# A two-layer hybrid decoder in fp32: one more FFN tile by seven products, the gate unit in two passes, and four changed orders

## What is computed

```python
def hybrid_layer(x, ...):
    h = rmsnorm(x, norm_mix)
    z = h @ w_in
    (rq, rk, rv, rg, pu, mq, mk, mv, mo, mi, mf) = jnp.split(z, offs, axis=-1)
    y_ret = retention(rq, rk, rv, rg, positions, ret_gn)
    y_pool = pool_mix(pu, pool_w, pool_scale)
    y_ml = mlstm(mq, mk, mv, mo, mi, mf, conv_w, conv_b, b_igate, b_fgate, mlstm_gn)
    x = x + jnp.concatenate([y_ret, y_pool, y_ml], axis=-1) @ w_out
    h = rmsnorm(x, norm_ffn)
    gu = h @ w_gate_up
    x = x + (jax.nn.silu(gu[..., :D_FF]) * gu[..., D_FF:]) @ w_down
    hp = rmsnorm(x, norm_ple)
    x = x + jax.nn.sigmoid(hp @ w_ple_gate) * (p_i @ w_ple_proj)
    return x
```

## Time and profile before

| | us |
|---|---|
| three runs | 2525.21, 2525.93, 2527.05 |
| median | 2525.93 |
| the profiled execution | 2527.18 |
| its span, first to last instruction | 2525.1 |
| PE busy (matmul) | 2485.7 |
| POOL busy | 992.1 |
| DVE busy | 1238.0 |
| ACT busy | 853.7 |

### The profile page before, as it was taken

How to read it: one execution, slowest core, us unless ns; L and a number is a source line. 1 busy time by engine, 2 the same in 40 slices (tenths; PEclk the granted TensorE clock), 3 DMA queues, 4 the chain that set the end, 5 groups by cost and what they waited for, 6 DMA issues and landing times.

```text
span 2525.1 us, 29697 instructions
## 1 busy us (share of the span) xinstructions
PE 2485.7 (98%) x11844; PEld 2052.7 (81%) x11844; DVE 1238.0 (49%) x1746; ACT 853.7 (34%) x1237; POOL 992.1 (39%) x596
## 2 busy tenths in 40 slices
PE   7999999999999999999999999999999999999997
PEld 5888788888888878888888888888888888888885
DVE  7856756454333352332585667546443333423335
ACT  4221225433333341234333121334333333322253
POOL 3211112177788742212121111222877887222220
PEclk9999999999999999999999999999999999999998
DMA  4322223122322252311142112311223223422111
GB/s 157 93 67 51 71 63 109 34 92 76 96 79 76 82 202 80 104 50 50 42 145 80 51 47 67 101 60 66 76 76 95 80 76 101 164 104 73 51 50 67
DMA packets 62904, 208.64 MB, mean 83 GB/s; under 512 B 8872, under 2 KB 17320, under 8 KB 58416
## 3 DMA queue, kind: packets, MB, share of 16 engines
q1 hardware_dynamic: 34848, 120.60, 15.2%
q10 hardware_dynamic: 27920, 86.16, 9.9%
HBM read 161.08 MB, written 32.54 MB: 77 GB/s over the span
## 4 chain that ended last, share of the span: by engine, by line
PE 97%; DVE 1%; ACT 1%; DMA 1%; issue 0%; POOL 0%; ACTq 0%; DVEq 0%; POOLq 0%
PE proj L1908 20%; PE proj L1910 20%; PE proj L1909 20%; PE proj L2002 5%; PE proj L2004 5%; PE proj L2003 5%; PE aux L2002 5%; PE aux L2004 5%; PE aux L2003 5%; PE aux L2046 1%; PE aux L2146 1%; PE aux L2137 1%; PE aux L2127 0%; PE aux L2232 0%; PE aux L2237 0%
## 5 line engine op out<-in xcount | busy, mean ns | idle before, releaser
L1859 POOL TENSOR_TENSOR w_lo<-w_raw,w_hi 128x1024 fp32r<-128x1024 f32 (+1 forms) x145 | 366.9, 2531 | 1312.2 <-ACT w_hi L1440 1312.0
L1908 PE MATMUL proj<-h_hi,w_hi 128*128 128x512 f32 x1792 | 711.9, 397 | 12.8 <-DVE h_lo L612 12.8
L1909 PE MATMUL proj<-h_hi,w_lo 128*128 128x512 f32 x1792 | 700.5, 391 | 0.0
L1910 PE MATMUL proj<-h_lo,w_hi 128*128 128x512 f32 x1792 | 700.4, 391 | 0.0
L1908 PEld LDWEIGHTS proj<-h_hi,w_hi 128*128 128x128 f32 x1792 | 338.2, 189 | 86.8 <-issue 16.5
L1909 PEld LDWEIGHTS proj<-h_hi,w_lo 128*128 128x128 f32 x1792 | 338.4, 189 | 71.8 <-issue 3.4
L1910 PEld LDWEIGHTS proj<-h_lo,w_hi 128*128 128x128 f32 x1792 | 338.1, 189 | 71.0
L1440 ACT ACTIVATE w_hi<-w_raw 128x1024 fp32r<-128x1024 f32 (+1 forms) x143 | 147.0, 1030 | 448.2 <-PE proj L1910 340.3
L1001 DVE TENSOR_TENSOR x<-x,proj 128x512 f32<-128x512 f32 x128 | 87.7, 687 | 407.3 <-PE proj L1910 407.1
L1866 POOL TENSOR_TENSOR w_lo<-w_raw,w_hi 128x512 fp32r<-128x512 f32 x120 | 183.6, 1531 | 88.5 <-ACT w_hi L1426 88.5
L1866 POOL TENSOR_TENSOR w_lo<-turns,w_hi 128x512 fp32r<-128x512 f32 x120 | 180.4, 1504 | 62.9 <-ACT w_hi L1426 62.9
(11 more groups left out here) (280 smaller groups left out, 4052.1 us busy)
## 6 DMA issues: line engine op xcount, KB each, us to landing
w_raw<-weights SPq DMA_DIRECT2D x170, 512.0 KB, 3.7
act_spill<-act ACTq DMA_DIRECT2D x44, 512.0 KB, 5.5
turns<-weights SPq DMA_DIRECT2D x40, 512.0 KB, 4.3
h_whole<-act_spill ACTq DMA_DIRECT2D x12, 1024.0 KB, 8.5
ffn_b_whole<-act_spill ACTq DMA_DIRECT2D x8, 1024.0 KB, 5.8
w_raw<-weights SPq DMA_DIRECT2D x16, 384.0 KB, 3.1
rows<-ret_qkv ACTq DMA_DIRECT2D x40, 128.0 KB, 2.3
x<-x_in ACTq DMA_DIRECT2D x8, 512.0 KB, 8.5
```

The lines of the kernel that those rows point to most:

```text
L1859: g.tensor_tensor(wlo[:, slot, 0:n], w, whi[:, slot, 0:n].bitcast(F32), ALU.subtract).then_inc(weights_ready.sem, 1)
L1908: pe.matmul(out, wh, rhi, start=first, stop=False)
L1909: pe.matmul(out, wl, rhi, start=False, stop=False)
L1910: return pe.matmul(out, wh, rlo, start=False, stop=final)
```

## The change

- **FFN.** `NSTD` goes from 2 to 1, so that 21 tiles are blocks. Block 0 now comes after one plain tile. Its tile of raw weights comes from the two `turns` slots, and the three banks of block 0 are those of `aux` in place of `proj`. An odd number of blocks leaves one half slot of the ring out at the start.
- **Third token sum.** DVE makes `t3` and the low parts of sum 1 ahead of `plain_up`. ACT makes the high parts of the fourth sum, and of operands 4 and 5, after the first product of block 0.
- **Gate unit.** Unit 0's weights have 64 columns at most, so the low parts are put into the columns 64 to 127 of `w_hi` (`gate_low`), and `two_passes` multiplies both with `h_hi` and then with `h_lo`. PSUM then has two parts, which DVE reads in two instructions and adds in a third.
- **Four orders.** POOL's split of unit 2 waits for the sum of squares in place of `h_lo`; ACT's high parts of activations 2 and 3 in the last block come one product later; the last token sum is made by PE from the sum of the first squares and the last two squares themselves; and DVE's adding of those two goes.

The core of the diff:

```diff
-NSTD = 2
+NSTD = 1
@@ plan_weights
             if u == U_DN:
+                block_turn = 2 * (NBS % 2)
+                at += NBS % 2
@@ vector, evacuate
                 if u == U_GATES:
-                    src, scale, dst = src[0:64], scale[0:64], mix[0:64, 0, sl]
+                    v.tensor_tensor(mix[0:64, 0, sl], src[0:64], scale[0:64], ALU.mult).then_inc(vec_step.sem, 1)
+                    step_at(L)
+                    src, scale, dst = src[64:128], scale[64:128], mix[0:64, 2, sl]
@@ vector, gate_rows_1
+                v.tensor_tensor(mix[0:64, 0, :], mix[0:64, 0, :], mix[0:64, 2, :], ALU.add).then_inc(vec_step.sem, 1)
@@ vector, ple_gates, last layer
                     gate_out(L, 15)
-                    gate_square(L, 14)
-                    gate_square(L, 15)
@@ vector, ffn
                         t_low(L, 0, 1)
+                        t3(L)
+                        t_low(L, 1, 0)
                         plain_up(L, 0)
-                        t_low(L, 1, 0)
-                        t3(L)
                         t_low(L, 2, 2)
-                        plain_gate(L, 1)
-                        plain_up(L, 1)
                         t_low(L, 3, 3)
@@ scalar, ffn_blocks
+                        if k == 0:
+                            a.wait_ge(unit_done.sem, unit_done.at(L, U_DN))
+                            t_high(L, 3, 3, 8)
+                            highs_ahead(L, 4)
+                            highs_ahead(L, 5)
...
-                        if last and 2 <= i <= 5:
-                            act_high(L, 2 * i - 4)
-                            act_high(L, 2 * i - 3)
+                        if last:
+                            for f in {2: (0, 1), 4: (2, 3, 4, 5), 5: (6, 7)}.get(i, ()):
+                                act_high(L, f)
@@ scalar, ffn
-                        units_high(L, U_FFN + 2)
                         t_high(L, 0, 1, 4)
                         plain_silu(L, 0)
-                        units_high(L, U_FFN + 3)
+                        highs_ahead(L, 0)
+                        highs_ahead(L, 1)
                         t_high(L, 1, 0, 0)
                         t_high(L, 2, 2, 12)
...
                         highs_ahead(L, 2)
                         highs_ahead(L, 3)
@@ gpsimd, split
+            def gate_low(hi, whole):
+                hi3 = hi.rearrange("p (k c) -> p k c", c=P)
+                whole3 = whole.rearrange("p (k c) -> p k c", c=P)
+                return g.tensor_tensor(hi3[:, :, 64:128], whole3[:, :, 0:64], hi3[:, :, 0:64].bitcast(F32), ALU.subtract)
...
                     if u == RING - 1:
-                        g.wait_ge(first_lo, KC)
+                        g.wait_ge(first_sum, KC - 1)
@@ tensor
+            def two_passes(out, slot, col, rhi, rlo, first, final):
+                both = whi[:, slot, col:col + P]
+                pe.matmul(out, both, rhi, start=first, stop=False)
+                return pe.matmul(out, both, rlo, start=False, stop=final)
...
+                passes = two_passes if u == U_GATES else three_passes
@@ tensor, end of the program
-            sums(DEPTH, -16, 0, (1,))
+            last_row = ("row", 0, 1)
+            pe.wait_ge(sq_added.sem, sq_added.at(DEPTH, -2))
+            pe.wait_ge(aux_read(last_row), aux_free_at(DEPTH, last_row))
+            pe.matmul(abank(last_row), mean_all, acc[:, 1, :], start=True, stop=False)
+            for j in (14, 15):
+                pe.wait_ge(sq_made.sem, sq_made.at(DEPTH, j - 15))
+                ins = pe.matmul(abank(last_row), mean_all, sqr[:, j % 2, :], start=False, stop=j == 15)
+            ins.then_inc(aux_done.sem, 1)
```

More of the change, by code:

```diff
@@ L185 @@
 AUX, AUX_FILLS, AUX_PER_BANK = plan_aux()
-VEC_STEPS = 271
+VEC_STEPS = 274
 OUT_LAST = [m for m in range(4, KC)] + [m for m in range(4)]
@@ L1496, in ffn_blocks @@
                             a.wait_ge(act_stored.sem, act_stored.at(L, 16 * (NSTD + b - 1)))
-                            a.activation(act_t[:, b % 2, 0, :], x_bank, ACT.Copy).then_inc(copied.sem, 1)
+                            a.activation(act_t[:, (NSTD + b) % 2, 0, :], x_bank, ACT.Copy).then_inc(copied.sem, 1)
+                        if k == 0:
[3 more added lines that the diff above has]
+                            highs_ahead(L, 5)
                         if i == 2:
-                            a.activation(act_t[:, b % 2, 1, :], x_bank, ACT.Copy).then_inc(copied.sem, 1)
+                            a.activation(act_t[:, (NSTD + b) % 2, 1, :], x_bank, ACT.Copy).then_inc(copied.sem, 1)
                         if i == 3:
@@ L1846, in split @@
                         g.wait_ge(first_w, 2 * q + 1)
-                        ins = g.tensor_tensor(wlo[:, 0, hs(q)], w[:, hs(q)], whi[:, 0, hs(q)].bitcast(F32), ALU.subtract)
+                        ins = gate_low(whi[:, 0, hs(q)], w[:, hs(q)])
                         ins.then_inc(first_w if q == 0 else weights_ready.sem, 1)
@@ L1858, in split @@
                     g.wait_ge(unit_hi.sem, unit_hi.at(L, u + 1))
+                if u == U_GATES:
+                    gate_low(whi[:, slot, 0:n], w).then_inc(weights_ready.sem, 1)
+                    return
                 g.tensor_tensor(wlo[:, slot, 0:n], w, whi[:, slot, 0:n].bitcast(F32),
@@ L1917, in product @@
                         ready(i, k)
-                    last = three_passes(out, slot_w, wk + col, rhi(k), rlo(k), i == 0, i == len(ks) - 1)
+                    last = passes(out, slot_w, wk + col, rhi(k), rlo(k), i == 0, i == len(ks) - 1)
                 return last
@@ L2012, in fill_read @@
                     pe.wait_ge(emptied[bank(u, k % 2)].sem, emptied_at(L, u, k % 2))
-                if b == 0:
+                if b == 1:
                     fill_read(0)
-                elif b == 1:
+                elif b == 0:
                     for name in (("row", 1, 0), ("row", 1, 1)):
```

19 lines of the change are left out of this document (6 added, 13 removed).

## The result

The changed kernel takes 2537.96 us (median of 7 runs, 2534.73 to 2541.87); the kernel before, run beside it, took 2527.05 (7 runs, 2523.68 to 2530.87). The ratio is 1.0041, 95% interval 1.0031 to 1.0051: slower by 0.4%. The forecast was 2520, faster. The profiled execution took 2539.96, its span 2538.2, which is 13.1 us over the span before.

The account below looks back on a forecast made before the run. TensorE was taken to bound the kernel, busy 2485.7 of 2525.1 us. From the profiled 2527.2, gains of 14.7 and a new wait of 9.0 gave 2521.5, so about 2520 for the median; range 2508 to 2536.

Parts of the forecast that it names:

- Matmuls removed: Whole kernel: a block has 12 matmuls fewer per layer than a plain tile, 24 x 0.226 = 5.4 us less.
- Start: Start of layer 0: sums of squares no longer held (-3.5), `h_lo` starts earlier (-0.6); together -4.1 us, bounds -3.4 and -7.
- No gain of clock: First token sums of layer 0: PE still waits about 3.6 us, so no gain from its clock was counted.
- Gate unit of layer 1: Layer 1's gate unit: one pass fewer saves 3.6 us, partly lost to waiting; -2.6 us left, bounds -1.5 and -3.6.
- Down projection: Layer 0's down projection: new order of high parts removes PE's wait; -1.8 us, bounds 0 and -2.2.
- End: End of the kernel: DVE's second adding leaves the chain; -0.8 us, bounds 0 and -1.8.
- The new wait: FFN start, block 0: POOL and DVE exclude each other, delaying products; at least 2.5 us, taken as 4.5 per layer, +9.0.
- Rival 1: FFN start: POOL gets the first turn, the two engines alternate, `gate_second` late; 11 us per layer, 2533, slower; chance 0.28.

Follow-up runs that it names:

- kernel 5: Changed kernel with GpSimd's low parts of blocks 0 and 1 and sums of block 1 cut to 64 of 512 columns; 2509.97 us, one execution.
- kernels 1: Changed kernel without its FFN part (`NSTD = 2`, old order at the FFN's start); 2515.61 us, ratio 0.9948 to the kernel before.
- 3: Changed kernel with GpSimd's work on block 1 held until VectorE has made the last low part of block 0's token sums; 2519.12 us, ratio 0.9963.
- 6: Changed kernel with GpSimd's work on block 1 held only until the low parts of the third token sum are made; 2528.33 us, ratio 1.000.
- 8: Kernel before with only GpSimd's split of unit 2 at the start moved behind VectorE's sums of squares; 2520.83 us, one execution.
- 11: Changed kernel with block 1 held behind the fourth token sum and the retention's third unit's low part behind VectorE's eight scalings; 2515.74 us.

## Why the prediction was wrong

It had the right mechanism in a rival and the wrong one in the forecast. For the profiled execution it gave -5.7 and the measurement +13.1, 18.8 apart; 17.8 of these are the one step below that failed. Point by point:

- **Matmuls removed, -5.4: right.** 12 a layer are worth 2.72 (kernel 5), 0.227 each. An estimate by the Trainium skill's figure (TensorE: Matmul & The Clock Gate, Back-to-back issue gap) is 3.1 for both layers. The measurement decides for the row: 5.44.
- **Start, -4.1: right in its two steps, short by the clock.** -4.75 after; the late split by itself -3.6 (the 3.5 of the working), the gates -0.9 (0.6 in the working). "No gain of clock" was wrong: the four token sums took 2.53, where undisturbed ones take 1.88 and three took 2.90 before, 0.9 more was gained behind them in this profile, and 2.5 in others (kernels 1, 3, 6, 8 and 11); with these 2.5 it comes to the bound of -7. The gates' extra VectorE instructions cost nothing that shows.
- **Gate unit of layer 1, -2.6: right.** 1.82 in the turn and 0.62 behind it, 2.4.
- **Down projection, -1.8: right in that profile** (422.63 to 420.65, 2.0). But that wait was not a fixed item of the kernel: with the old order it is 0 to 2 us, from profile to profile.
- **End, -0.8: too small by half.** It gave 1.6. I took only the second adding off the chain and left the first; both squares now go straight from ScalarE into TensorE.
- **The new wait, +4.5 per layer: the step that failed.** It is 13.4 per layer. The text walked the case in which GpSimd is kept out until 510.9, as in the earlier trace rows: one wait of 5.7 at product 3, behind GpSimd's low part, and "later ones hold no more". It took a value between this and the bound (which is 3.1 and not 2.5 by its own numbers: 529.2 + 1.2 - 527.3). The runs showed another path. Product 3 was 1.1 late, and the other 12.3 come behind it, most at the products 5 and 7, which wait for VectorE's `h_lo` and `silu_g`. For GpSimd was not kept out for long: it asked at 502.43, was let in when `t3` began, at 503.7, and from then each engine's next instruction stood ready when the other's ended, up to 534.3, so that four low parts took 6.81 in place of 2.48. I had set a chance of 0.28 on this without asking how long either order lasts: a kept-out run ends with the run, an alternation ends only when one side's work does.
- **Who is let in: not settled.** VectorE's run had no gap at 503.7, so an unbroken run is not what keeps GpSimd out. In the kernel before, GpSimd was kept out twice per layer (not once, as the text has it): at 506.01, and in the row below, where 1.0 of the 2.30 is waiting. Both times it got in when VectorE came to an instruction that reads PSUM (507.79 and 520.28), and at 503.7 when VectorE went over to `t3`; but at 535.56 it got in between two of the same low parts. What decides this stays open.

```profile
519.22 2.30 POOL L1866 TENSOR_TENSOR w_lo<-w_raw,w_hi 128x512 fp32r<-128x512 f32 x1 [9.09 <-ACT w_hi L1426]
```

- **The rule on who blocks whom.** The Trainium skill (SBUF - State Buffer, Who interferes with whom) says that the pair is an exclusive lock and that whoever issues first has it for the whole instruction. It says the latter of VectorE's two-port modes, and of instructions with two inputs in SBUF that they contend with GpSimd's reads. The trace agrees on the blocking. It does not agree on the order at 502.43, where by the recorded starts two of VectorE's instructions that began later, at 502.47 and 503.07, still went first.
- **Rival 1, 11 per layer: right in kind, and in size partly by luck.** `gate_second` came 27.2 behind block 0's first product, where the rival has 27.1 (538 less 510.9), and product 7, behind `silu_g`, started 11.6 late. But `t3` ended 1.9 behind that first product and not 4.1, the products 3 and 5 were 1.1 and 3.1 late and not 2 and 5, and GpSimd had nine instructions of block 1 in by then where seven were counted: errors that cancel. Its price left out the half clock in product 7 behind the long wait, 1.7. It gave 2533; the measured 2538 lies 2 us above the range's upper end, 2536.
- **Unforeseen:** the mLSTM stage. The prediction summed against one profiled execution as if the parts not edited were constant. They were not: 17.3 to 21.3 us for one piece of code, and 0 to 2.0 for another. Of the 13.1 us between the two profiles, 3.3 are of that kind.

## What to carry to other kernels

When two engines exclude each other on an access, count the pairs and not the work: a stretch in which both always have something ready costs the longer queue nearly a full turn of the other for each instruction (1.1 us of 1.25 here), so an engine that works ahead on what nobody needs yet is an expense, and one wait that holds it back can be worth more than the instructions saved (here 16 us against 5.4). Before a cover is removed, ask which engine will use the freed time first. And compare the unedited stages of several profiles before summing against one: where two engines' work only just misses, the clock can decide which form a run takes, as in the 20 stretches here.

## What the runs showed of the hardware

- One instruction of VectorE (128x512, both inputs in SBUF, 0.60 alone) and one of GpSimd (1.25 alone) take 1.7 a pair, in turn, for some 30 us (503.7 to 534.3), as long as both have one ready. With GpSimd's at 64 columns four low parts still took 3.00 in place of 2.48.
- Who goes first when both have one ready does not follow from the order of asking: GpSimd, asking at 502.43, was passed by two of VectorE's, and at 535.56 in the kernel before it was let in at once behind the current one.
- VectorE's instructions with one input in PSUM are not held: `act<-proj,rstd` took 1.27 for two, beside GpSimd's three of 516.77, where `act<-act,silu_g` took 2.37 for two. The Trainium skill says so (SBUF - State Buffer, Who interferes with whom: at most one input in SBUF, no contention), and this trace agrees; the prediction counted only the others, rightly.
- A higher TensorE clock made a stage longer: 21.3 with the clock up throughout, 18.0 with a part at half, because everything but TensorE kept its speed and a low part arrived 1.7 us sooner, into VectorE's run. With that low part held back the order is the usual one: 15.8 with the clock up, 16.3 and more with a part at half.
